# A decoder step on one core: down projection waits per block, index head weights inside the key block, constants awaited at the first rotation

## The reference, cut to what matters

```python
a_q, a_k, a_v, i_q, i_k, i_w, b_q, b_k, b_v = split_cols(h @ w_in, AB_SECTIONS)
i_q = rope(i_q.reshape(bsz, t, IDX_HEADS, IDX_DIM), pos)      # 8 heads of 64
i_k = rope(i_k.reshape(bsz, t, 1, IDX_DIM), pos)              # one key of 64 for a token
i_w = i_w * IDX_HEADS ** -0.5                                 # 8 head weights for a token
...
logits = jnp.einsum('bthd,bsd->bths', q_idx, k_idx) * IDX_DIM ** -0.5
score = jnp.einsum('bth,bths->bts', w_idx, jax.nn.relu(logits))
_, sel = lax.top_k(score, n_sel)                              # the keys that are attended to
...
def sq_relu_mlp(h, w_up, w_down):                             # hidden 4096
    u = jax.nn.relu(h @ w_up)
    return (u * u) @ w_down
```

## Time and profile before

| | us |
|---|---|
| time, median of 3 runs | 2179.78 (2178.3 to 2184.92) |
| the profiled execution's own time | 2179.58 |
| its span, first to last instruction | 2177.9 |
| TensorE busy | 1971.5 (91%) |
| VectorE busy | 735.6 (34%) |
| ScalarE busy | 421.8 (19%) |
| GpSimd busy | 267.5 (12%) |

### The profile page before, as it was taken

One profiled execution on the slowest core, in us unless ns is written; L12 is line 12 of the kernel. 1 busy time (PEld: TensorE's weight loads), 2 busy tenths in 40 slices (PEclk: granted clock), 3 DMA queues, 4 the chain that ended last, 5 costly groups with the idle time before them and its releaser, 6 DMA issues.

```text
span 2177.9 us, 32241 instructions
## 1 busy us (share of the span) xinstructions
PE 1971.5 (91%) x11246; PEld 1426.5 (65%) x11246; DVE 735.6 (34%) x1600; ACT 421.8 (19%) x766; POOL 267.5 (12%) x482
## 2 busy tenths in 40 slices
PE   7899967877778999999999899888798999999996
PEld 5467524544556777777777675455576777777774
DVE  2379875556501411110000422567504111100002
ACT  1221024454501200000000300344413000000000
POOL 3002121221120000000000000233200000000000
PEclk9999987988779999999999999999999999999998
DMA  7111083877562122212222220699611222222221
GB/s 233 57 42 49 1 344 112 315 264 253 219 223 68 58 67 67 67 58 68 67 67 67 87 66 31 236 373 362 234 58 49 68 67 67 67 68 67 67 67 53
DMA packets 95092, 264.48 MB, mean 121 GB/s; under 512 B 13649, under 2 KB 20050, under 8 KB 94354
## 3 DMA queue, kind: packets, MB, share of 16 engines
q0 software_dynamic: 46560, 167.80, 22.6%
q1 hardware_dynamic: 44146, 88.86, 11.6%
q10 hardware_dynamic: 4288, 6.51, 0.9%
HBM read 255.30 MB, written 7.82 MB: 121 GB/s over the span
## 4 chain that ended last, share of the span: by engine, by line
PE 77%; DVE 6%; DMA 5%; ACT 3%; issue 3%; DVEq 3%; ACTq 2%; SPq 1%; POOLq 0%; POOL 0%; PEldq 0%
PE ps L490 60%; PE ps L546 3%; DMA arena<-in_kv_c 3%; DMA arena<-in_kv_ab 2%; DVE arena L1325 1%; PE ps L730 1%; DMA arena<-in_lambdas 1%; DVEq L1329 1%; ACTq L333 1%; PE ps L576 1%; PE ps L706 1%; PE ps L666 1%; PE ps L716 1%; PE ps L880 1%; PE ps L647 1%
## 5 line engine op out<-in xcount | busy, mean ns | idle before, releaser
L490 PE MATMUL ps<-hs,wring 128*128 128x288 f32 x3520 | 874.8, 411 | 25.7 <-ACT hs L997 17.1
L490 PEld LDWEIGHTS ps<-hs,wring 128*128 128x128 f32 x3520 | 676.3, 193 | 221.5 <-issue 21.0
L490 PE MATMUL ps<-arena,wring 128*128 128x288 f32 x2048 | 500.4, 408 | 5.7 <-DVE arena L1359 5.7
L490 PEld LDWEIGHTS ps<-arena,wring 128*128 128x128 f32 x2048 | 391.5, 191 | 114.6 <-issue 6.6
L417 POOL DMA_DIRECT2D wring<-in_weights x170 | 90.2, 531 | 1332.3 <-PE ps L490 1332.0
L1357 DVE TENSOR_TENSOR arena<-arena,norm 128x576 f32 x64 | 48.5, 758 | 371.6 <-ACT arena L1016 365.3
L1314 DVE TENSOR_TENSOR norm<-norm 128x576 f32<-128x576 f32 x24 | 18.2, 759 | 448.6 <-ACT norm L1007 448.6
L1016 ACT ACTIVATE arena<-ps 128x576 f32 (+1 forms) x76 | 49.4, 650 | 527.3 <-PE ps L490 527.3
L1007 ACT ACTIVATE norm<-ps 128x576 f32<-128x576 f32 x32 | 20.8, 650 | 633.0 <-PE ps L490 633.0
L348 POOL DMA_DIRECT2D arena<-in_kv_ab x128 | 68.8, 538 | 312.4 <-PE ps L716 156.3
L1441 DVE TENSOR_SCALAR_CACHE_REDUCE arena<-arena,isel 128x1088 f32<-128x1088 f32 (+1 forms) x124 | 91.3, 793 | 4.9 <-issue 2.5
(11 more groups left out here) (247 smaller groups left out, 1748.5 us busy)
## 6 DMA issues: line engine op xcount, KB each, us to landing
wring<-in_weights POOLq DMA_DIRECT2D x174, 512.0 KB, 3.8
arena<-in_kv_ab SPq DMA_DIRECT2D x128, 320.0 KB, 5.4
arena<-in_kv_ab POOLq DMA_DIRECT2D x128, 320.0 KB, 6.5
arena<-in_kv_c SPq DMA_DIRECT2D x128, 256.0 KB, 5.0
arena<-in_kv_c POOLq DMA_DIRECT2D x128, 256.0 KB, 5.6
arena<-in_w_v_ab SPq DMA_DIRECT2D x1, 2592.0 KB, 27.5
xs<-in_x_t SPq DMA_DIRECT2D x4, 576.0 KB, 8.9
out_y_t<-xs SPq DMA_DIRECT2D x4, 576.0 KB, 2.8
```

The costliest lines, as they stand in the source:

```text
L490: mm = pe.matmul(out[:, h * 512:h * 512 + TH], wring[:, slot, k], inp[:, b * KD + k, h * TH:(h + 1) * TH], start=(b == 0 and k == 0), stop ...
```

## The change

1. The down projection's wait for all 32 squared blocks goes. Its first output waits, ahead of each of its four weight blocks, for the 8 input blocks that this weight block meets (`u0`). The first two outputs are written out (`peel=2`), the other six run in a loop as before.
2. The index key's block comes first (`IK, IQ = 0, 1`). It holds the key once, in rows 0 to 63, the 8 head weights in rows 64 to 71, and zeros. ScalarE evicts the head weights from it ahead of the block itself; VectorE copies the rotated key to rows 64 to 127. The 16 products of the head weights and their wait for the value weights go; the transposes stand after the rotation that follows the third output. VectorE's rotations are written out; its clearing of tiles stands ahead of them, its copies of the head weights after the third. TensorE waits for `i_staged` at S0 alone, and `ORDER_I` begins with P0 P1 P2.
3. TensorE waits for `loads` ahead of its first rotation and not ahead of the first output.
4. ScalarE issues the store of the index key ahead of the fifth eviction.
5. The value weights (640 columns) go to the place of ring slots 2 and 3, `kx[1]` to that of slots 0 and 1. TensorE frees slots 0 and 1 after the sample scores, slots 2 and 3 after the values.

```diff
-        IQ, IK, AQ, AK, BQ, BK = 0, 4, 5, 9, 10, 14
-        N_I = IK + 1
+        IK, IQ, AQ, AK, BQ, BK = 0, 1, 5, 9, 10, 14
+        N_I = IQ + 4
-        wv = area(RNG0, KD * VW).rearrange("p (k w) -> p k w", k=KD)
+        wv = area(RNG0 + 2 * GW, KD * 640).rearrange("p (k w) -> p k w", k=KD)
-        kx = [area(tr0, 4096), area(RNG0 + KD * VW, 4096)]
+        kx = [area(tr0, 4096), area(RNG0, 4096)]
-        ORDER_I = "S0 P0 P1 S1 P2 S2 P3 P4 S3 P5 S4 P6 P7 S5 P8 S6 P9 P10 S7 P11".split()
+        ORDER_I = "P0 P1 P2 S0 P3 S1 P4 S2 P5 S3 P6 S4 P7 S5 P8 S6 P9 P10 S7 P11".split()
...
                     pe.wait_ge(w_landed[slot], landed(g, gstat, b))
+                    if u0 is not None:
+                        pe.wait_ge(relu_sq, u0 + KD * (b + 1))
...
+                if b == 0:
+                    pe.wait_ge(i_staged, 1)
...
             first_stats()
-            pe.wait_ge(loads, 48)
-            dense(G_AB, O_AB, N_I, hs, peel=N_I, after=rotate(O_AB, 0, qk), h0=0)
-            rotate(O_AB, 0, qk)(N_I, N_I, True)
-            pe.wait_ge(wv_landed, 16)
-            for k in range(KD):
-                for h in range(2):
-                    mm = pe.matmul(ps[3][0:8, h * 512:h * 512 + TH], wv[:, k, 640:648], hs[:, k, h * TH:(h + 1) * TH],
-                                   start=(k == 0), stop=(k == KD - 1))
-            mm.then_inc(iw_a, 1)
+            rotate_i = rotate(O_AB, 0, qk)
+            def after_i(j, jstat, static):
+                if j == 1:
+                    pe.wait_ge(loads, 48)
+                rotate_i(j, jstat, static)
+                if j == 2:
+                    pe.wait_ge(iw_b, 1)
+                    for t in range(4):
+                        pe.transpose(ps[3][:, t * 8:(t + 1) * 8], iw_t[:, t * P:(t + 1) * P], C["ident"][0:8, 0:8])
+                    pe.matmul(ps[3][:, 512:512 + NS], C["expand"][0:8, :], iw_t[:, SEQ:T], start=True, stop=True).then_inc(iw_a, 1)
+            dense(G_AB, O_AB, N_I, hs, peel=N_I, after=after_i, h0=0)
+            rotate_i(N_I, N_I, True)
...
             pe.wait_ge(i_relu, NB)
+            for slot in range(2):
+                pe.sem_inc(kv_free[slot], 4)
...
-            for slot in range(KVR):
+            for slot in range(2, KVR):
                 pe.sem_inc(kv_free[slot], 4)
...
-                pe.wait_ge(relu_sq, N_UP * (layer + 1))
-                dense(g_dn, o_dn, KD, U, sub=4)
+                dense(g_dn, o_dn, KD, U, sub=4, peel=2, u0=N_UP * layer)
...
+                if j == IK:
+                    act.activation(two(iw_t), halves(ps[j % 2])[64:72], ACT.Copy, scale=8 ** -0.5).then_inc(iw_b, 1)
                 act.activation(two(qk[:, j]), halves(ps[j % 2]), ACT.Copy).then_inc(dense_out, 1)
...
+                if j == 3:
+                    act.wait_ge(rope_done, 1)
+                    act.dma_start(ik_t, qk[0:64, IK, :]).then_inc(ik_stored, 16)
```

More of the change, by code:

```diff
@@ L475, in norm_stats, with output @@
                 mm.then_inc(stat_done, 1)
-            def output(g, o, gstat, ostat, inp, sub, static, h0=None):
+            def output(g, o, gstat, ostat, inp, sub, static, h0=None, u0=None):
                 if not static or ostat >= 2:
@@ L497, in landed, with dense @@
                 return g[0] * (g[1] // RING * 16) + 16 * ((gstat + b) // RING + 1)
-            def dense(g0, o0, n_out, inp, sub=1, peel=0, after=None, h0=None):
+            def dense(g0, o0, n_out, inp, sub=1, peel=0, after=None, h0=None, u0=None):
                 per = 4 if sub == 1 else 2
@@ L505, in straight @@
                     for j in range(j0, j1):
-                        output(g0 + j * sub, o0 + j, g0 + j * sub, o0 + j, inp, sub, True, h0 if j == 0 else None)
+                        output(g0 + j * sub, o0 + j, g0 + j * sub, o0 + j, inp, sub, True,
+                               h0 if j == 0 else None, u0 if j == 0 else None)
                         if after:
@@ L580, in _ @@
             first_stats()
-            pe.wait_ge(loads, 48)
-            dense(G_AB, O_AB, N_I, hs, peel=N_I, after=rotate(O_AB, 0, qk), h0=0)
-            rotate(O_AB, 0, qk)(N_I, N_I, True)
-            pe.wait_ge(wv_landed, 16)
-            for k in range(KD):
-                for h in range(2):
-                    mm = pe.matmul(ps[3][0:8, h * 512:h * 512 + TH], wv[:, k, 640:648], hs[:, k, h * TH:(h + 1) * TH],
-                                   start=(k == 0), stop=(k == KD - 1))
-            mm.then_inc(iw_a, 1)
-            pe.wait_ge(dense_out, N_I)
[L593 to L597, removed]
+            rotate_i = rotate(O_AB, 0, qk)
[10 more added lines that the diff above has]
+            rotate_i(N_I, N_I, True)
+            pe.wait_ge(dense_out, N_I)
             pe.wait_ge(rope_done, N_I)
-            pe.wait_ge(i_staged, 1)
             for what in ORDER_I:
@@ L1408, in _ @@
                 dve.tensor_copy(pen_p[:, OFF[i] + i * P:OFF[i] + (i + 1) * P], C["tri"])
-            dve.wait_ge(iw_a, 2)
-            dve.tensor_copy(vt[:, 0:4, 640:648], ps[0][:, 0:32].rearrange("p (t h) -> p t h", t=4))
-            dve.tensor_tensor(w2, ps[0][:, 512:512 + NS], C["qmask"], ALU.mult).then_inc(iw_b, 1)
-            dve.drain()
+            for j in range(N_I):
+                dve.wait_ge(rot_done, j + 1)
+                dve.tensor_tensor(two(rope_t), halves(ps[2]), two(C["sin"]), ALU.mult)
+                dve.tensor_tensor(qk[:, j], qk[:, j], C["cos"], ALU.mult)
+                dve.drain()
+                if j == IK:
+                    dve.tensor_tensor(qk[:, j], qk[:, j], rope_t, ALU.add)
+                    dve.drain()
+                    dve.tensor_copy(qk[64:128, j], qk[0:64, j]).then_inc(rope_done, 1)
+                else:
+                    dve.tensor_tensor(qk[:, j], qk[:, j], rope_t, ALU.add).then_inc(rope_done, 1)
+                dve.drain()
+                if j == 2:
+                    dve.wait_ge(iw_a, 1)
+                    dve.tensor_copy(vt[:, 0:4, 640:648], ps[3][:, 0:32].rearrange("p (t h) -> p t h", t=4))
+                    dve.tensor_tensor(w2, ps[3][:, 512:512 + NS], C["qmask"], ALU.mult)
+                    dve.drain()
+                    for s in range(2):
+                        for half in range(2):
+                            rows = slice(64 * half, 64 * half + 64)
+                            dve.tensor_copy(wz[rows].rearrange("k (p s) x -> k p s x", s=2)[:, :, s, 16 * s + 8 * half:16 * s + 8 * half + 8],
+                                            w2[rows].rearrange("k (p s q) -> k p s q", s=2, q=NQ)[:, :, s, :])
             for s in range(2):
@@ L1418, in _ @@
                                         qk[64 * o:64 * o + 64, IQ:IQ + 4, SEQ:T].rearrange("k c (p s q) -> k p c s q", s=2, q=NQ)[:, :, :, s, :])
-                    rows = slice(64 * half, 64 * half + 64)
-                    dve.tensor_copy(wz[rows].rearrange("k (p s) x -> k p s x", s=2)[:, :, s, 16 * s + 8 * half:16 * s + 8 * half + 8],
-                                    w2[rows].rearrange("k (p s q) -> k p s q", s=2, q=NQ)[:, :, s, :])
             dve.drain()
```

11 lines of the change are left out of this document (3 added, 8 removed).

## The result

The changed kernel takes 2158.49 us (median, 2153.41 to 2161.53) against 2181.61 us for the kernel before beside it: a ratio of 0.9892, 95% interval 0.9866 to 0.9917. Measured once more beside other runs of the kernel before it gave 2154.64 us against 2179.80, 0.9885 [0.9866, 0.9903]. The forecast was 2157.9. The execution that was profiled took 2153.41 us (span 2151.5) and is the fastest of its four; that of the kernel before took 2179.58.

A forecast was written before the change was run, and what follows sets the result against it. ScalarE paces the start, VectorE's search the way to attention, and gaps precede the down projections. Gains of 3.2 + 8.8 + 0.8 + 8.9 = 21.7 us from 2179.58 give 2157.9 us, range 2150 to 2168.

The forecast's parts named there:

- The down projections: Both layers' gaps of 2.85 us and 1.6 us of low clock behind each go: 8.9 us, lower bound 4.7.
- Rival 1: Down projections: the end of TensorE's loop costs what the gap hides, gain only 12.8 us, 2166.8; chance 0.12.
- The index scores: Fifth eviction to index sums: 36.6 us instead of 45.4, gaining 8.8, bounds 6.9 and 10.0.
- rival 2: Index scores: clock stays low, some 2 us more per sample unit distance, gain becomes loss of 5, 2171.9; chance 0.07.
- the 8.0 forecast: Index scores: first sample unit S0 begins about 8.0 us after the fifth eviction's start, 9 in the lower-gain bound.
- the 0.9 us counted for a slow large product: Index scores: half the low-clock excess of the first sample unit's large product, 3.75 us instead of 1.98.
- upper bound of 10.0: Index scores: largest gain expected for this stage, with none of the low clock.
- The start: Up to the fifth eviction: it begins at 71.3 instead of 74.46, gaining 3.2 us, bounds 1.6 and 4.8.
- the 31.0: Start: first output's end, 21.6 + 7.8 + 1.6 for lost clock; 29.4 if the clock holds.
- The attention's start: First key product's 0.81 us wait for keys goes: 0.8 us gained, bounds 0 and 2.4.
- Rival 3: Attention: clock falls to 0.75, its work 29 us longer, 2187; chance 0.05.
- rival 4: Attention: early keys carry through, removing waits at its start and as much again, 4 us more, 2154; chance 0.10.

The follow-up runs named there:

- e1: Kernel before with only the down projection's part (waits per weight block, two outputs written out): 2169.47 us, ratio 0.9948.
- e4: Changed kernel with TensorE's wait for the constants ahead of the first output again: ratio 0.9872 to the kernel before.
- after_again: The changed kernel run and profiled a second time, nothing altered: ratio 0.9885 to the kernel before.
- before_again: The kernel before run and profiled once more, nothing altered; fifth eviction at 72.77 us, no ratio given.
- e3: Changed kernel with all four ring slots freed only after the values, as before the change: ratio 0.9892 to the kernel before.
- e5: Changed kernel with the old `ORDER_I`, S0 first: ratio 0.9878 to the kernel before.
- e6: Changed kernel with ScalarE's 32 index key loads issued by GpSimd instead: ratio 0.9877 to the kernel before.
- e8: Changed kernel with index key loads on GpSimd and five unused products ahead of the first output: ratio 0.9908 to the kernel before.

## Why the prediction held, step by step

**The down projections: 8.9 forecast, 9.2 found.** Both gaps and the clock loss behind them went, 2 x 2.85 + 1.70 + 1.79. Each length shrank by a little more than the 1.6 us that had been read from the granted clock. Rival 1 fell: the row at 941.12 has no idle time ahead of it, nor has that of e1.

**The index scores: 8.8 forecast, 8.7 found.** From the fifth eviction to the sums 45.44 became 36.71, forecast 36.6. With all profiles of either kind: 45.44, 45.37 and 46.82 (mean 45.9) with the old start, 36.71 and 38.02 (mean 37.4) in the changed kernel's two, 8.5 apart. The sample units lie 3.4 us apart as forecast (80.53 to 104.38 over seven: 3.41), so rival 2 fell. Inside the sum two terms were off and cancelled. The first sample unit begins 9.2 us after the fifth eviction (9.6 in the second profile), past the 8.0 forecast and its bound of 9, because the three prompt units ahead of it take 3.88 us instead of some 2.4: they run at half clock, which is back when the sample unit runs (windows as in the earlier trace rows):

```profile
76.00:78.00 2.00, 1.28 (x6) 1.19 (x8) 1.84 (x7) 0.01 (x1) 0.00 (x0) 0.50 0.11 33
78.00:80.00 2.00, 2.00 (x8) 0.73 (x6) 1.47 (x5) 1.32 (x2) 0.00 (x0) 0.50 0.12 29
80.00:82.00 2.00, 2.00 (x8) 0.75 (x5) 1.52 (x3) 1.10 (x2) 0.00 (x0) 0.96 0.12 29
```

Against that, the 0.9 us counted for a slow large product wasn't paid in this profile (1.99 us); in the second it was (2.96 instead of 1.98). The prediction's upper bound of 10.0 for this stage doesn't follow from its terms: without any low clock they give 8.8 + 0.9 = 9.7.

**The start: 3.2 forecast; right in the profile, wrong in its cause.** The fifth eviction at 71.29 is the 71.3 of the sum, but only because the first output ends 0.5 us later than the 31.0 (31.46) and the stretch from there to the fifth eviction is 0.5 shorter than its 40.28 (39.83). And the profile of before that the sum was made against had its constants landing 1.6 to 1.8 us later than the other old-start profiles. Over the three profiles with the old start the fifth eviction lies at 72.4 on average, in the changed kernel's two at 70.8: 1.6 us, the prediction's lower bound. The moved wait alone gives about 1.1 us at TensorE's start by the four profiles that wait there (e4 above), and nothing when the constants land with VectorE's first block, as in e4. At full clock the old start is even ahead at the fifth eviction, 69.99 (e1) against 70.35 (after_again), since the change adds work on ScalarE; with the first output slowed it is 72.77 (before_again, 10.93 us) against 71.29 (9.72 us). The step that doesn't hold is "VectorE begins them at 20.83 ..., so TensorE can begin at 21.6 instead of 24.4": the start was right, the 24.4 was one execution's, and the others with this wait began at 22.6 to 22.8. What an earlier start gives is also uncertain through the clock, which the prediction had left open between 29.4 and 31.0; from 21.6 these are outputs of 7.8 and 9.4 us, and the two profiles of the changed kernel took 8.03 and 9.72. The Trainium skill ("TensorE: Matmul & The Clock Gate", section "What's actually happening") says that the gate's observation runs freely and that the same kernel may therefore show different numbers of slow products in different runs. The two profiles agree: the same gap of 2.61 us cost 1.7 us in one and nothing in the other.

**The attention's start: 0.8 forecast, 0.4 found.** The waits of 0.81 and 1.59 us for keys went, and the first 64-column product of the attention begins 33.08 us after its start instead of 33.45. By e3 nothing of it reaches the time.

**The attention's length: not forecast.** It gave 6.4 us in the first profile and 5.3 in the second, and without it the change would have given less than forecast. TensorE's work is the same, 3068 or 3069 records, so one window over the whole stage shows how its time splits into busy and idle; the column behind GpSimd's busy time is the granted clock. The kernel before:

```profile
286.94:634.39 347.45, 264.42 (x3069) 164.22 (x3069) 185.93 (x351) 148.21 (x256) 70.78 (x132) 0.84 0.69 252
```

The changed kernel, first profile:

```profile
275.07:616.14 341.07, 264.78 (x3068) 163.92 (x3069) 186.08 (x351) 148.28 (x256) 70.78 (x132) 0.84 0.69 247
```

The changed kernel, second profile (after_again):

```profile
275.45:617.60 342.15, 261.66 (x3069) 163.36 (x3069) 186.08 (x351) 148.12 (x256) 70.79 (x132) 0.85 0.69 249
```

In the first profile clock and busy time are those of before, and the 6.4 us are idle time (76.29 us instead of 83.03). So the clock doesn't explain them, though e3's theory had put them down to it. In the second profile 2.8 of the 5.3 us are busy time at a slightly higher clock and 2.5 are idle time. Of the idle time, TensorE's waits for cached keys and values (`in_kv_ab`, sums of the list of waits) are 15.3 us before, 11.3 and 13.3 in the changed kernel's two profiles and 17.7 in e3, which is as short as they are, with a busy time of 260.67 us. Over all profiles the length is 347.3 to 347.5 in the three with the old start and 340.3 to 347.2 in the nine with the new one, 343.2 on average. So some 4 us may belong to the change, or three old profiles happen to be alike; e3 speaks against the slots and e5 (344.15) against the list as the one cause, with one profile each, and the cause stays open. Rival 3, a fallen clock in the attention, didn't come: 0.84 before, 0.84 and 0.85 after. Of rival 4, the early keys, the shorter waits are there, but e3 leaves nothing of them that the time shows.

**The sum** came out right partly by luck, because two errors cancel. With averages over the profiles, attention begins 10.1 us earlier (285.3 to 275.3 for the three old starts and the changed kernel's two) where 12.8 were forecast, the down projections give 9.2 where 8.9 were, and the attention's length some 4 where nothing was: 23, and the two measurements are 23.1 and 25.2 us. The forecast's 21.7 counted 2.7 us too many ahead of the attention and lacked some 4 within it.

## What to carry to other kernels

Where an engine waits for the last of many inputs although its first work needs only some, let it wait piece by piece: the gap goes, and the low clock behind it too, which was over a third of the gain here (3.5 of 9.2 us). A chain that goes round several engines at a stage's end can be shortened by computing its inputs in an output that exists already: the head weights as 8 spare rows of the key's block cost one eviction of 0.64 us and took 8.33 us of products out of the chain. A wait that ended last in one profile may have done so by chance, so look for it in a second execution before counting its whole length as a gain.

## What the runs showed that was not expected

- The same gap of 2.61 us on TensorE, between the first statistics and the projection, was followed by a low clock in five profiles (starts at 21.46 to 21.90, first output 9.72 or 9.73 us) and by none in two (22.09 and 22.61, 8.03 and 8.04 us). One of 3.28 us cost nothing (e1), one of 3.67 did (before_again, 10.93 us). The length of the gap alone doesn't say it. The seven profiles with the low clock are those whose statistics ended at 18.85 to 19.29 us, the three without it those where they ended at 19.47 to 20.01; no run moves that end by itself, so this is an observation and no cause. Where the gap was filled the clock stayed full, also in e8, whose statistics ended at 18.96.
- One issue of a page of index keys holds ScalarE for 1.1 to 1.2 us (8.75 to 9.46 us for eight), more than an eviction of 576 columns (0.65 us). Issuing them between its evictions, ScalarE paced the outputs, with TensorE idle for 4.84 us ahead of the last rotation; with these loads on GpSimd the fifth eviction came 5.3 us earlier.
- The landing of the last constants varied by 1.8 us between executions of the same kernel (19.1 and 17.3 us from issue).
- Layer 0's attention varied by 7 us between kernels whose work in it is the same: TensorE's busy time in it by 8.4 us (260.04 to 268.48), its idle time by 7.4 (75.68 to 83.03); a milestone gained by 3 to 4 us ahead of it was not to be seen in the median of six runs (e6, e8).
